# The closing stage of a hybrid mixer and expert block: column halves, sums in PSUM, rows scaled by GpSimd, a store in halves

## The reference, cut to what matters

```python
h = rmsnorm(x, norm_gains[l, 2]) * (1.0 + sc2) + sh2
y = hierarchical_moe(h, ...)          # sum over experts, two per token
x = x + gt2 * rmsnorm(y, norm_gains[l, 3])
```

## Time and profile before

| what | value |
|---|---|
| median of 3 runs | 1114.98 us (1114.25 to 1116.09) |
| time of the profiled execution | 1113.32 us |
| span of the profiled execution | 1111.8 us |
| mean granted clock of TensorE in it | 0.983 of 2.4 GHz |
| busy: PE, PEld, DVE, ACT, POOL | 94%, 52%, 59%, 28%, 13% |
| HBM read, written | 274.52 MB, 4.21 MB |

### The profile page before, as it was taken

The page is one execution under the profiler, slowest core; times in us unless marked ns, Lnnn a source line. Parts: engine busy times, 40 slices in busy tenths (PEclk is TensorE's granted clock), DMA queues, the critical chain, the costliest instruction groups (busy, mean ns, idle before and its releaser), DMA issues.

```text
span 1111.8 us, 17976 instructions
## 1 busy us (share of the span) xinstructions
PE 1040.0 (94%) x7315; PEld 581.8 (52%) x7315; DVE 657.3 (59%) x1124; ACT 313.3 (28%) x479; POOL 145.6 (13%) x206
## 2 busy tenths in 40 slices
PE   3999999999999999999997899999999999889993
PEld 1588588755556775546884344444444333333341
DVE  2477867444466441137347577777777765666675
ACT  4342462466641222144351011111111101110114
POOL 0100000323320100222601100000000000001002
PEclk9999999999999999999998999999999999999996
DMA  9676312214210002433439999999999999999993
GB/s 343 236 254 219 112 61 92 76 63 165 76 76 2 4 4 78 153 143 124 155 128 378 354 398 401 402 405 397 404 404 409 405 404 394 405 397 403 412 420 151
DMA packets 67667, 275.39 MB, mean 248 GB/s; under 512 B 7760, under 2 KB 17274, under 8 KB 43034
## 3 DMA queue, kind: packets, MB, share of 16 engines
q1 hardware_dynamic: 62832, 263.84, 61.4%
q10 hardware_dynamic: 2218, 6.52, 1.6%
q0 software_dynamic: 2560, 4.20, 1.4%
HBM read 274.52 MB, written 4.21 MB: 251 GB/s over the span
## 4 chain that ended last, share of the span: by engine, by line
PE 60%; SPq 22%; DMA 5%; DVE 5%; ACT 4%; issue 2%; POOL 1%; ACTq 0%; POOLq 0%; DVEq 0%
SPq L455 15%; PE ps L2100 9%; PE ps L1765 7%; PE ps L2119 5%; SPq L459 5%; PE ps L1632 4%; PE ps L1633 4%; PE ps L1634 4%; PE ps L1776 3%; DMA arena<-in_w_up 2%; PE ps L2084 2%; SPq L463 2%; DMA ring<-in_w_in 2%; PE ps L1877 2%; PE ps L2019 1%
## 5 line engine op out<-in xcount | busy, mean ns | idle before, releaser
L1464 DVE TENSOR_TENSOR arena<-arena,ps 128x1024 f32<-128x1024 f32 x124 | 145.5, 1214 | 52.5 <-PE ps L2084 52.5
L2100 PE MATMUL ps<-arena 128*64 128x512 f32 x672 | 154.5, 602 | 11.0 <-DMA arena<-in_w_up 10.3
L1765 PE MATMUL ps<-arena,ring 128*128 128x512 f32 x256 | 118.6, 604 | 0.0
L2100 PEld LDWEIGHTS ps<-arena 128*64 128x64 f32 x672 | 47.8, 138 | 105.2 <-issue 101.5
L983 ACT ACTIVATE results<-ps,ST 64x512 fp32r<-64x512 f32 x64 | 43.7, 682 | 183.6 <-PE ps L2119 183.2
L2100 PE MATMUL ps<-ring,arena 128*64 128x512 f32 x352 | 81.4, 606 | 6.5 <-DMA ring<-in_w_up 4.3
L978 ACT ACTIVATE arena<-ps 128x256 f32<-128x256 f32 x32 | 12.3, 383 | 242.4 <-PE ps L2100 242.4
L2084 PE MATMUL ps<-results,back 128*128 128x512 f32 x256 | 77.5, 426 | 3.2 <-DVE results L1471 3.2
L2119 PE MATMUL ps<-arena 128*64 128x512 f32 x336 | 76.7, 598 | 1.5 <-DMA arena<-in_w_down 1.5
L1632 PE MATMUL ps<-h_upper,w_upper 128*128 128x512 f32 (+1 forms) x184 | 73.6, 400 | 4.8 <-POOL h_lower_first L580 4.5
L1471 DVE SCALAR_TENSOR_TENSOR results<-ps,ST,results 64x512 fp32r<-64x512 f32 x64 | 48.0, 750 | 47.3 <-ACT results L983 46.8
(11 more groups left out here) (394 smaller groups left out, 1717.4 us busy)
## 6 DMA issues: line engine op xcount, KB each, us to landing
arena<-in_w_up SPq DMA_DIRECT2D x84, 1024.0 KB, 27.6
ring<-in_w_up SPq DMA_DIRECT2D x44, 1024.0 KB, 27.4
ring<-in_w_down SPq DMA_DIRECT2D x11, 2048.0 KB, 32.4
arena<-in_w_down SPq DMA_DIRECT2D x11, 2048.0 KB, 30.0
arena<-in_w_down SPq DMA_DIRECT2D x20, 1024.0 KB, 26.9
ring<-in_w_mod SPq DMA_DIRECT2D x6, 2048.0 KB, 9.2
arena<-in_w_mod SPq DMA_DIRECT2D x6, 2048.0 KB, 9.4
ring<-in_w_in SPq DMA_DIRECT2D x6, 2048.0 KB, 8.3
```

The costliest lines, as they stand in the source:

```text
L1464: TT(two_banks(acc[:, t, :]), two_banks(acc[:, t, :]), ps[:, BACK_BANK[t]:BACK_BANK[t] + 2, :], ALU.add).then_inc(back_added, 1)
L1765: last = mm(ps[:, bank, :], w[:, k, P * (n % 2):P * (n % 2) + P], hT[:, k, :], start=(k == 0), stop=(k == KD - 1))
L2100: last = mm(ps[64 * hf:64 * hf + 64, UP_BANK, :].rearrange("p (m n) -> p m n", m=2), hgT[:, k, :], up_pair(u, k)[:, :, 256 * hf:256 * hf + ...
```

## The change

- The last block's two column halves are passed on one by one: ScalarE raises `yo_upper` after each, VectorE raises `yo_ready` after each. TensorE makes the half-0 products of tiles 0 to 2, then the half-1 products.
- For tiles 0 and 3 (`SUMMED_BY_PE`) TensorE itself puts the running sum into PSUM, by a product of the identity with `acc` in f32 (`carried_sums`), ahead of the last block's products, which accumulate on it. For tile 0 that comes before the wait for `yo_ready`, for tile 3 after the products of tiles 0 to 2. VectorE's adds of tiles 0 and 3 go.
- ScalarE loads its table right behind the last SiLU, and scales no residual rows. It takes tile 0's square sum when `fin_sum` is raised, tile 3's when `fin_sum` and `fin_row` are.
- GpSimd scales the residual rows of all four tiles as soon as they have landed, then adds those of tiles 0 and 1.
- VectorE: add 1, scale 0, add 2, the product of tile 3 with the row of gains (into tile 0's banks), scale 1, scale 2 (into PSUM), the residual of tile 2, and for tile 3 two instructions of 512 columns that multiply by the inverse root and add the residual.
- SyncE stores tile 2 when VectorE has done it, and tile 3 as two stores of 512 columns (rows of 2 KB).

```diff
--- before.py
+++ after.py
@@ -347,6 +347,7 @@
         hrow_in = [sem(f"hrow_in{u}") for u in range(NSET)]
         UP_BANK, DOWN_BANK = 2, 3
         BACK_BANK, FIN_BANK = (4, 6, 4, 6), (4, 6, 0, 2)
+        SUMMED_BY_PE = (0, 3)
         fin_ss, fin_sum, fin_row, fin_rstd, first_ready, fin_ready = (sem(n) for n in (
             "fin_ss", "fin_sum", "fin_row", "fin_rstd", "first_ready", "fin_ready"))
         out_stored = sem("out_stored")
@@ -567,10 +568,13 @@
             sp.sem_inc(register_pass, 1)
             for t in range(NT):
                 sp.dma_start(x1_rows[t], h2_dram[P * t:P * t + P, :]).then_inc(h2_moved, 16)
-            for t in range(NT):
-                sp.wait_ge(*((first_ready, t + 1) if t < NT - 1 else (fin_ready, 1)))
+            for t in range(NT - 1):
+                sp.wait_ge(*((first_ready, t + 1) if t < 2 else (fin_ready, 1)))
                 sp.dma_start(out[0, P * t:P * t + P, :], acc[:, t, :]).then_inc(out_stored, 16)
-            sp.wait_ge(out_stored, 16 * NT)
+            for h in range(2):
+                sp.wait_ge(fin_ready, h + 2)
+                sp.dma_start(out[0, P * (NT - 1):T, 512 * h:512 * h + 512], acc[:, NT - 1, 512 * h:512 * h + 512]).then_inc(out_stored, 16)
+            sp.wait_ge(out_stored, 16 * (NT + 1))
 
 
         @block.gpsimd
@@ -655,8 +659,11 @@
                 pool.sem_inc(register_pass, 1)
                 gather_rows(u, idx_i[:, LAST + u:LAST + u + 1])
 
-            for t in range(NT - 1):
-                pool.wait_ge(fin_row, t + 1)
+            pool.wait_ge(h2_moved, 2 * 16 * NT)
+            for t in range(NT):
+                nc.gpsimd.tensor_scalar(x1_rows[t], x1_rows[t], std2[:, t:t + 1], None, ALU.mult).then_inc(x1_back, 1)
+            for t in range(2):
+                pool.wait_ge(fin_row, 2 * t + 1)
                 pool.wait_ge(x1_back, t + 1)
                 nc.gpsimd.tensor_tensor(acc[:, t, :], acc[:, t, :], x1_rows[t], ALU.add).then_inc(first_ready, 1)
 
@@ -972,16 +979,19 @@
             nc.scalar.preload_act_table_set("silu_and_others")
             again = act.value_load(nblk_i[0:1, 20:21], min_val=LOOPED // NSET - 1, max_val=(LOOPED + MAXO) // NSET - 1)
 
-            def expert_act(blocks, weight, loaded=None):
+            def expert_act(blocks, weight, loaded=None, final=False):
 
                 act.wait_ge(up_done, blocks)
                 A(sil, ps[:, UP_BANK, 0:256], ACT.Silu).then_inc(sil_ready, 1)
+                if final:
+                    nc.scalar.preload_act_table_set("natural_log_exp_and_others")
                 if loaded is not None:
                     act.wait_ge(w_now_ready, loaded)
                 act.wait_ge(down_done, blocks)
                 for a, h in ((0, 0), (HD, 512)):
                     last = A(yo[a:a + HD, h:h + 512], ps[a:a + HD, DOWN_BANK, :], ACT.Copy, scale=weight[a:a + HD, :])
-                last.then_inc(yo_upper, 1)
+                    if final or a:
+                        last.then_inc(yo_upper, 1)
 
             for u in range(NSET):
                 expert_act(u + 1, w_now[:, u:u + 1], NSET)
@@ -989,27 +999,15 @@
                 for u in range(NSET):
                     expert_act(NSET * it + (NSET + u + 1), w_now[:, u:u + 1], NSET * it + (NSET + u + 1))
             expert_act(NSET * again + (NSET + 1), w_slot[:, LAST:LAST + 1])
-            expert_act(NSET * again + (NSET + 2), w_slot[:, LAST + 1:LAST + 2])
-            act.wait_ge(h2_moved, 2 * 16 * NT)
-
-            def x1_scaled(t):
-                A(x1_rows[t], x1_rows[t], ACT.Copy, scale=std2[:, t:t + 1]).then_inc(x1_back, 1)
-
-            x1_scaled(0)
-            x1_scaled(1)
-            nc.scalar.preload_act_table_set("natural_log_exp_and_others")
-
-            def square_sum(t):
-
-                act.wait_ge(fin_ss, t + 1)
+            expert_act(NSET * again + (NSET + 2), w_slot[:, LAST + 1:LAST + 2], final=True)
+
+            for t in range(NT):
+                act.wait_ge(*((fin_sum, t + 1) if t in SUMMED_BY_PE else (fin_ss, t)))
+                if t == NT - 1:
+                    act.wait_ge(fin_row, 2)
                 link(A(two_banks(fin_sq), whole(t), ACT.Square, accum_out=V("ss", 12 + t)))
                 link(A(V("ss", 12 + t), V("ss", 12 + t), ACT.Ln, scale=1.0 / D, bias=eps_rms))
                 A(V("rs", 12 + t), V("ss", 12 + t), ACT.Exp, scale=-0.5).then_inc(fin_rstd, 1)
-
-            for t in range(NT):
-                square_sum(t)
-                if t == 0:
-                    x1_scaled(2)
 
 
         @block.vector
@@ -1463,11 +1461,14 @@
                 dve.wait_ge(back_done, sent)
                 TT(two_banks(acc[:, t, :]), two_banks(acc[:, t, :]), ps[:, BACK_BANK[t]:BACK_BANK[t] + 2, :], ALU.add).then_inc(back_added, 1)
 
-            def yo_lower(blocks, weight):
+            def yo_lower(blocks, weight, final=False):
 
                 dve.wait_ge(yo_upper, blocks)
                 for a, h in ((0, 0), (HD, 512)):
                     o = HD - a
+                    if final and a:
+                        last.then_inc(yo_ready, 1)
+                        dve.wait_ge(yo_upper, blocks + 1)
                     last = STT(yo[o:o + HD, h:h + 512], ps[a:a + HD, DOWN_BANK, :], weight[a:a + HD, :],
                                yo[a:a + HD, h:h + 512].bitcast(F32), ALU.mult, ALU.subtract)
                 last.then_inc(yo_ready, 1)
@@ -1505,7 +1506,7 @@
                 if not first:
                     add_back(2, NT * before - 1)
                     add_back(3, NT * before)
-                yo_lower(before + 1, weight)
+                yo_lower(before + 1, weight, last)
 
             rows_turned_in(1)
             nc.vector.reciprocal(std2, V("rs", 8, NT))
@@ -1539,21 +1540,27 @@
                 dve.wait_ge(fin_sum, t + 1)
                 TT(whole(t), two_banks(acc[:, t, :]), whole(t), ALU.add).then_inc(fin_ss, 1)
 
-            def scaled_row(t):
+            def scaled_row(t, to):
 
                 dve.wait_ge(fin_rstd, t + 1)
-                return STT(two_banks(acc[:, t, :]), whole(t), V("rs", 12 + t), row2, ALU.mult, ALU.mult)
-
-            last_added(0)
+                return STT(to, whole(t), V("rs", 12 + t), row2, ALU.mult, ALU.mult)
+
             last_added(1)
-            scaled_row(0).then_inc(fin_row, 1)
+            scaled_row(0, two_banks(acc[:, 0, :])).then_inc(fin_row, 1)
             last_added(2)
-            scaled_row(1).then_inc(fin_row, 1)
-            last_added(3)
-            scaled_row(2).then_inc(fin_row, 1)
-            link(scaled_row(3))
-            dve.wait_ge(h2_moved, 2 * 16 * NT)
-            STT(acc[:, 3, :], x1_rows[3], std2[:, 3:4], acc[:, 3, :], ALU.mult, ALU.add).then_inc(fin_ready, 1)
+            dve.wait_ge(fin_sum, NT)
+            dve.wait_ge(fin_row, 1)
+            TT(whole(0), whole(3), row2, ALU.mult).then_inc(fin_row, 1)
+            scaled_row(1, two_banks(acc[:, 1, :])).then_inc(fin_row, 1)
+            link(scaled_row(2, whole(2)))
+            dve.wait_ge(x1_back, 3)
+            TT(two_banks(acc[:, 2, :]), whole(2), two_banks(x1_rows[2]), ALU.add).then_inc(fin_ready, 1)
+            dve.wait_ge(fin_rstd, NT)
+            dve.wait_ge(x1_back, NT)
+            dve.wait_ge(fin_row, 2)
+            for h in range(2):
+                STT(acc[:, 3, 512 * h:512 * h + 512], ps[:, FIN_BANK[0] + h, :], V("rs", 12 + 3), x1_rows[3][:, 512 * h:512 * h + 512],
+                    ALU.mult, ALU.add).then_inc(fin_ready, 1)
 
 
         @block.tensor
@@ -2157,11 +2164,30 @@
                     expert(u, it + 1, NSET * it + (NSET + u))
             expert(0, again + 1, NSET * again + NSET)
             expert(1, again + 1, NSET * again + (NSET + 1), last=True)
-            pe.wait_ge(yo_ready, NSET * again + (NSET + 2))
+            def carried_sums(t):
+
+                for h in range(2):
+                    mm(ps[:, FIN_BANK[t] + h, :], ident, acc[:, t, 512 * h:512 * h + 512], start=True, stop=False)
+
+            def last_block(t, h):
+
+                return mm(ps[:, FIN_BANK[t] + h, :], back[:, 1, P * t:P * t + P], yo[:, 512 * h:512 * h + 512],
+                          start=t not in SUMMED_BY_PE, stop=True)
+
             pe.wait_ge(back_added, NT * NSET * again + (NT * (NSET + 1) + 1))
             pe.sem_inc(register_pass, 1)
-            for t in range(NT):
-                send_back(1, t, FIN_BANK[t]).then_inc(fin_sum, 1)
+            carried_sums(0)
+            pe.wait_ge(yo_ready, NSET * again + (NSET + 2))
+            pe.sem_inc(register_pass, 1)
+            for t in range(3):
+                last_block(t, 0)
+            pe.wait_ge(yo_ready, NSET * again + (NSET + 3))
+            pe.sem_inc(register_pass, 1)
+            for t in range(3):
+                last_block(t, 1).then_inc(fin_sum, 1)
+            carried_sums(3)
+            last_block(3, 0)
+            last_block(3, 1).then_inc(fin_sum, 1)
 
 
```

## The result

The changed kernel is slower: 1117.58 us in the median of 18 runs, against 1114.7 for the kernel before beside it; the ratio is 1.0023, with a 95% interval of 1.0016 to 1.0030. That is 1.8 to 3.3 us more, where 2.75 less was forecast. One of the 18 runs, 1753.67 us at a mean granted clock of 0.558, is left out of the ratio.

A forecast was written before the change was run, and what follows sets the result against it. VectorE was taken to bound the closing stage, the DMA queue after the change: stores from 1103.07 reach their last byte at 1108.04, the span ends at 1109.05, 2.75 us less, so 1112.2 us; range 1111.2 to 1114.4.

The forecast's parts named there:

- I take 1.1: GpSimd's scaling of residual rows: 1.1 us per row, between bounds 1.04 (cast) and 4.3 (affine select), done at 1095.6.
- the cover: GpSimd's four scalings stay hidden ahead of its adds while a row costs less than 1.8 us.
- Halves and carried sums: Start of closing stage: halves gain 0.70 us, carried sums fill TensorE's idle time; first square sum at 1094.23, not 1096.87.
- rival 3: Reordering does not deliver (added waits, code tail, wrong order of starts): 0.8 us or more, 1113.0 to 1115.0; chance 0.10.
- VectorE's order: VectorE's closing instructions: 10.2 us in place of 11.6, last one done at 1104.50; last tile ready 3.8 us earlier.
- The clock: TensorE's closing products run at full clock, granted 1.00 to about 1097, because the engine no longer idles ahead of them.
- The stores: Closing DMA queue: tile 1 issued at 1103.07, then 2.27 + 1.30 + 1.30 and the split's price; last byte 1108.04, end 1.0 later.
- The price of the split: Tile 3's store in two halves: one more DMA taken as 0.1 us, bounds zero and 1.5.
- The residual rows have landed by 1091.2: Ahead of GpSimd's scalings: rows in place by about 1091.2, so scaling can begin then.
- Rival 4: GpSimd's scalings delay tile 1's store: 2.5 us per row decides, at 4.3 the kernel takes 1122.3; chance 0.06.
- The fixed 2.0 us per DMA: Closing stores: by this cost paid in series, the two halves would end some 4 us later than forecast.
- rival 1: Split stores leave gaps, each half paying its own start of 0.77: end 1.4 us later, 1113.6; chance 0.11.

The follow-up runs named there:

- pool_copy: Changed kernel with GpSimd's four scalings replaced by in-place copies of the same size, scaling left out: closing stage 17.9 us, ratio 0.9988 to the kernel before.
- no_halves: Changed kernel with GpSimd scaling only tiles 0 and 1 (ScalarE 2 and 3), and both last-block halves passed on together: closing stage 19.3 us.
- no_carried: Changed kernel with GpSimd scaling only tiles 0 and 1 (ScalarE 2 and 3), and VectorE adding all four tiles, no TensorE running sums: closing stage 20.4 us.
- whole_store: Changed kernel with GpSimd scaling only tiles 0 and 1 (ScalarE 2 and 3), and tile 3 stored in one piece: closing stage 17.6 us.
- split_rows: Changed kernel with GpSimd scaling the residual rows of tiles 0 and 1 only, ScalarE those of 2 and 3: 1112.57 us, ratio 0.9982 to the kernel before.
- tile1_halves: Changed kernel with ScalarE scaling rows of tiles 2 and 3, and GpSimd adding tile 1 in two separately stored halves: 1111.2 us, ratio 0.9962 to before.

## Why the prediction was wrong

The step that failed is one term of the sum: "I take 1.1, because the cast has the same size and one input". It measured 2.83. The bounds, 1.04 and 4.3, did hold it; the choice between them was by the wrong likeness. The cast has the size, the affine select has the kind of operation, and I let size decide; neither row gives 2.83. A third row of the same size, the two-tensor add at 2.33, was used for the adds only and not weighed here, though it already lies above the cover that I had stated, 1.8 us per row. At 2.83 the cover is gone: 4 x (2.83 - 1.8) = 4.1, with 0.35 for the late start, is the 4.4 by which the store of tile 1 was late. That the price alone makes the stage's loss is shown by pool_copy: with 1.04 in its place the stage is 17.9.

The rest, point by point:

- *Halves and carried sums.* Right: tile 0's square sum 0.12 sooner than forecast; the halves are worth 1.4 (no_halves), where rival 3 held it possible that they save nothing, and the carried sums 2.5 (no_carried).
- *VectorE's order.* Right to 0.04 us at its last instruction.
- *The clock.* Right: 1.00 through the closing products.
- *The stores.* Right in mechanism, and nearly in size: from the issue of tile 1's store to the end 4.97 + 1.0 forecast, 22.39 - 16.30 = 6.1 measured. What was wrong is when it was issued: 4.4 late, and the stage is 22.4 where 17.84 was forecast, 4.5 more. The price of the split was taken as 0.1; whole_store puts it at 0.3, on one trace.
- *The residual rows have landed by 1091.2.* Nearly: GpSimd starts 0.35 into the stage, not at 0.
- *Rival 4* named the mechanism, the queue and the price at which it decides (2.5 us). With 2.83 it gives 4 x (2.83 - 2.5) = 1.3, and 0.35 for the later start, 1.7 us slower; the stage measured 1.8. I gave it 0.06. It had a row for it and a row against it, and a threshold inside the bounds: that is no case for 6 in 100, and the range, which stopped at 1114.4, should have reached to it.
- *The Trainium skill* (GPSIMD Engine Reference, section 4.1 Engine selection) calls one-input work roughly line-rate. The copy agrees (1.04 us for 1024 columns); the tensor-scalar does not (2.83), and here the measurement decides. The second half of the rule sends elementwise work to VectorE; no run here gave it these rows. ScalarE took two of them in split_rows, at 1.15 and 1.13.
- *The fixed 2.0 us per DMA* that rival 1 takes from the Trainium skill (DMA: Bandwidth & Descriptors) stands there in the section Anatomy of one DMA, as a fit for DMAs issued by GpSimd, not in the section Bandwidth, and the stores here are SyncE's. Paid in series, rival 1 estimated, it would have made the end 4 us later; by split_rows against whole_store it costs 0.3.

## What to carry to other kernels

An operation that moves to another engine has to be priced by a row of the same operation on that engine; where there is none and the deciding price lies between the bounds, the range has to reach over it. Work placed ahead of a releaser in an engine's queue is free only until the releaser's new, earlier time: three scalings were hidden in the old order, and with the adds released 2.7 us sooner even three would not have been (an estimate), let alone the four that were put there. When the last stores leave back to back, the end is set by when that run starts, not by how finely the last tile is cut.

## What the runs showed of the hardware that was not expected

- GpSimd, 128x1024 f32 in SBUF: copy 1.04 us, product with a broadcast column 1.89, two-tensor add 2.33, tensor-scalar by a pointer 2.83 and by a constant 2.76. One input less made it slower, not faster. ScalarE does the scaling in 1.15.
- Stores issued one right behind the other took longer and longer to issue: 0.34, 0.42, 0.79 and 1.19 us in the kernel after. The last two are SyncE's half stores:

```profile
1110.57 0.79 SPq L576 DMA_DIRECT2D out<-arena  x1
```

```profile
1111.40 1.19 SPq L576 DMA_DIRECT2D out<-arena  x1
```

It is neither the half store as such nor the number of stores under way alone. In tile1_halves, where the two half stores of tile 1 come 1.2 us apart, they took 0.34 and 0.33. In whole_store the last store was issued 0.54 us after the issue before it had ended, with both earlier stores still moving or waiting, and took 0.33. What sets it was not tried; nothing waited for it here.
